# Which three experts are fixed ahead of routing, and a third shared step: 13 expert steps in place of 14

## The reference

```
g_sel = argmax(softmax(xf @ w_rg + b_rg))                 # one group of 4
in_group = e_logits of that group                         # 4 experts
top_w, top_i = top_k(softmax(in_group), 2); top_w /= sum(top_w)
h = silu(xf @ w_g[e]) * (xf @ w_u[e])                     # 1024 -> 256
out = sum over the two e of gate * (h @ w_d[e])           # 256 -> 1024
```

## Time and profile before

| | us |
|---|---|
| median of three runs | 541.12 |
| the profiled execution, its own time | 539.75 |
| its span, first to last instruction | 537.5 |
| TensorE busy | 518.3 (96%) |
| VectorE busy | 259.3 (48%) |
| GpSimd busy | 155.0 (29%) |
| ScalarE busy | 151.2 (28%) |
| granted TensorE clock, mean of the span | 0.993 |

### The profile page before, as it was taken

How to read it: one execution, slowest core, us unless ns; L and a number is a source line. 1 busy time by engine, 2 the same in 40 slices (tenths; PEclk the granted TensorE clock), 3 DMA queues, 4 the chain that set the end, 5 groups by cost and what they waited for, 6 DMA issues and landing times.

```text
span 537.5 us, 7583 instructions
## 1 busy us (share of the span) xinstructions
PE 518.3 (96%) x2798; PEld 322.0 (60%) x2798; DVE 259.3 (48%) x759; ACT 151.2 (28%) x293; POOL 155.0 (29%) x166
## 2 busy tenths in 40 slices
PE   7999999999999999999999999878999999999994
PEld 6777755554455454557544444557887768668841
DVE  3543465543024223342633276576746766663247
ACT  6332497721122222232222315410100111011132
POOL 3016000116000000000310020336777677777310
PEclk8999999999999999999999999999999999999998
DMA  9999997899900000007931022969998999999574
GB/s 289 357 330 353 340 312 312 306 388 370 333 4 1 0 0 1 1 1 284 382 112 64 39 66 87 382 190 402 364 355 282 365 370 364 365 377 368 124 197 179
DMA packets 47417, 126.50 MB, mean 235 GB/s; under 512 B 6654, under 2 KB 19358, under 8 KB 41234
## 3 DMA queue, kind: packets, MB, share of 16 engines
q1 hardware_dynamic: 30912, 99.36, 50.1%
q0 software_dynamic: 11408, 22.05, 15.0%
q10 hardware_dynamic: 5058, 4.58, 2.5%
HBM read 116.48 MB, written 17.30 MB: 249 GB/s over the span
## 4 chain that ended last, share of the span: by engine, by line
PE 82%; DMA 8%; DVE 5%; issue 2%; ACT 1%; POOL 0%; ACTq 0%; SPq 0%; POOLq 0%; DVEq 0%
PE psum L816 78%; DMA f_dram<-arena,add_tok 5%; PE psum L819 3%; DMA u_dram<-arena 2%; DVE arena L2386 1%; DVE x L2391 1%; DMA arena<-f_dram 1%; DMA hy<-in_c_sample_dram 1%; ACT arena L1502 1%; DVE arena L2187 0%; ACT L1502 0%; POOL f_dram L785 0%; DVE arena L2333 0%; ACT hy L1502 0%; POOL uT L774 0%
## 5 line engine op out<-in xcount | busy, mean ns | idle before, releaser
L816 PE MATMUL psum<-ring,uT 128*128 128x512 f32 (+1 forms) x384 | 126.5, 523 | 0.0
L816 PEld LDWEIGHTS psum<-ring,uT 128*128 128x128 f32 (+1 forms) x384 | 56.7, 173 | 60.0 <-issue 55.7
L1502 ACT ACTIVATE arena<-psum 128x512 f32<-128x512 f32 (+6 forms) x80 | 35.7, 476 | 168.2 <-PE psum L816 150.9
L816 PE MATMUL psum<-uT,ring 128*128 128x288 f32 x256 | 64.9, 411 | 0.1
L816 PEld LDWEIGHTS psum<-arena,ring 128*128 128x128 f32 x512 | 58.5, 192 | 5.9 <-issue 3.9
L816 PE MATMUL psum<-arena,ring 128*128 128x128 f32 x512 | 59.2, 276 | 2.7 <-DVE arena L2187 1.8
L754 POOL DMA_INDIRECT arena<-u_dram,part_tok x52 | 53.4, 1027 | 19.9 <-issue 14.3
L816 PEld LDWEIGHTS psum<-uT,ring 128*128 128x128 f32 x256 | 47.9, 190 | 16.2 <-issue 4.0
L816 PE MATMUL psum<-ring,arena 128*64 128x256 f32 (+2 forms) x192 | 50.6, 490 | 0.0
L785 POOL DMA_INDIRECT f_dram<-arena,add_tok x26 | 41.5, 1598 | 23.1 <-DMA f_dram<-arena,add_tok 13.2
L1502 ACT ACT_TABLE_LOAD x33 | 42.3, 1283 | 3.1 <-issue 2.1
(11 more groups left out here) (260 smaller groups left out, 613.4 us busy)
## 6 DMA issues: line engine op xcount, KB each, us to landing
ring<-in_w_mod_dram SPq DMA_DIRECT2D x24, 1024.0 KB, 11.5
ring<-in_w_exp_down_dram SPq DMA_DIRECT2D x12, 1024.0 KB, 13.4
ring<-in_w_exp_gate_dram SPq DMA_DIRECT2D x11, 1024.0 KB, 9.9
ring<-in_w_exp_up_dram SPq DMA_DIRECT2D x11, 1024.0 KB, 12.5
ring<-in_w_in_dram SPq DMA_DIRECT2D x10, 1024.0 KB, 10.2
ring<-in_w_out_dram SPq DMA_DIRECT2D x4, 1024.0 KB, 6.9
uT<-in_w_exp_gate_dram SPq DMA_DIRECT2D x4, 1024.0 KB, 14.2
f_dram<-in_consts_dram POOLq DMA_DIRECT2D x2, 1536.0 KB, 17.0
```

What stands on the lines that cost most here:

```text
L816: return nc.tensor.matmul(out, lhsT, rhs, start=first, stop=last)
L1502: return nc.scalar.activation(out, src, func, **kw).then_inc(done, 1)
```

## The change

Experts 13, 14 and 15 are fixed ahead of routing in place of 0, 1 and 2, and the ranked ones are experts 0 to 12, so column numbers shift by `SORTED` and the offset of `FIRST` goes away. Of the ranked ones, seven run alone and six share three steps, (7, 8), (9, 10) and (11, 12): 13 steps in all. Steps 4, 7 and 10 are pairs, where 5 and 9 were. `NST` and `BIG` (9, now 7) follow from the list. `LAST_AT` stays 7, a paired step now. In the new order of weights the 16th late piece is the first gate weights of step 7, in the cell of step 4's; the 28th to 31st are those of the pair in step 10, the 34th the gate weights of step 11.

```diff
-STEPS = [()] * FIRST + [(0,), (1,), (9, 10), (2,), (3,), (4,), (11, 12), (5,), (6,), (7,), (8,)]
+STEPS = [()] * FIRST + [(0,), (7, 8), (1,), (2,), (9, 10), (3,), (4,), (11, 12), (5,), (6,)]
...
                 if a < FIRST:
-                    return slice(a, a + 1)
+                    return slice(SORTED + a, SORTED + a + 1)
...
-                    chosen[at] = sp.value_load(order[0:1, at:at + 1], min_val=FIRST, max_val=NE - 1)
+                    chosen[at] = sp.value_load(order[0:1, at:at + 1], min_val=0, max_val=SORTED - 1)
...
-                          scale=gsl[e % 4][:, e:e + 1])
+                          scale=gsl[e % 4][:, SORTED + e:SORTED + e + 1])
...
-                link(v.tensor_tensor(out=masked, in0=rank1[:, :, FIRST:NE],
+                link(v.tensor_tensor(out=masked, in0=rank1[:, :, 0:SORTED],
...
-                        col = rank1[:, t, e:e + 1] if e < FIRST else ranks[e % 2][0][:, t:t + 1]
+                        col = (rank1[:, t, SORTED + e:SORTED + e + 1] if e < FIRST
+                               else ranks[e % 2][0][:, t:t + 1])
...
-                out=key, in0=bank[6][:, FIRST:NE], scalar=float(NE),
+                out=key, in0=bank[6][:, 0:SORTED], scalar=float(NE),
...
-                    v.tensor_scalar(order, ordf, float(FIRST - 1), None, ALU.add)\
+                    v.tensor_scalar(order, ordf, -1.0, None, ALU.add)\
...
-                    link(v.tensor_tensor(out=masked[:, 0], in0=gsl[e % 4][:, FIRST:NE], in1=mine,
+                    link(v.tensor_tensor(out=masked[:, 0], in0=gsl[e % 4][:, 0:SORTED], in1=mine,
```

More of the change, by code:

```diff
@@ L2460, in take_out @@
                         dve.wait_ge(s_gs[e % 2], 16 * (e // 2 + 1))
-                        v.tensor_scalar(eo[e % 2][:, 512:1024], bank[5], gsl[e % 4][:, e:e + 1],
+                        v.tensor_scalar(eo[e % 2][:, 512:1024], bank[5], gsl[e % 4][:, SORTED + e:SORTED + e + 1],
                                         None, ALU.mult).then_inc(s_eod, 1)
@@ L2556, in _ @@
                         ranks_of(STEPS[NST - 1][0], lastr)
-                        link(v.tensor_tensor(out=masked, in0=gates[:, :, FIRST:NE],
+                        link(v.tensor_tensor(out=masked, in0=gates[:, :, 0:SORTED],
                                              in1=mine.unsqueeze(1)
```

## The result

The changed kernel took 544.34 us in the median of four runs (543.60 to 545.41), the kernel before beside it 540.65 (540.13 to 541.88, four runs): ratio 1.0066, 95% interval 1.0039 to 1.0093. It is slower by 3.6 us, where 538.3 was forecast; the range ended at 543.6. The profiled execution was the longest of the four, 545.41 us, with a span of 543.5.

What follows compares the result with a forecast made beforehand. TensorE, the weight stream and the closing scatter-adds were taken to bind within some 7 us. Of TensorE's 9.3 us, half went in the stream; scatters landing 2.8 us earlier, off the 541.12 median, gave 538.3, range 535.8 to 543.6.

Steps and rivals of the forecast that it cites:

- TensorE's saving: Expert loop: two single steps out, one pair in, 10.8 us off TensorE's path, 9.3 left after VectorE's delay.
- the stall in step 1: Step 1: TensorE's down products wait for VectorE's slot comparisons and hidden values, 1.5 us on TensorE's path.
- The dip closes: DMA share around 399 to 421 us: early rows keep the weight queue full, recovering 3.3 us.
- the piece that mattered: The 34th late weight piece, step 11's gate weights: to land at 486.2 instead of 487.7.
- The prediction's row counts: Rows gathered and scattered up to 487.7 us: 1843 before, 1946 after, 103 more costing 1.8 us of DMA time.
- Step 11's gate weights are the 34th: Step 11's start: TensorE arrives at 482.7, waits for the 34th piece at 486.2; loop ends at 511.8, not 516.66.
- rival 2: Waits before steps 10 and 11: TensorE's clock falls there and the gain shrinks; chance 0.08.
- The tail: Closing scatter-adds: first issued at 499.2, last landing at 512.6 instead of 515.36, moving the finish 2.8 us earlier.
- Rival 1: Expert loop: stream keeps up, TensorE's saving arrives, end at 507.4, 3.8 to 5 us won, 536.5; chance 0.15.
- Rival 3: Weight stream: the DMA hole stays, 34th piece at 489.5, scatters land at 515.8, 541.1 us; chance 0.20.
- Rival 4: Step 10: the pair's scatters take 9.6 us each in the full stream, 545.3 us, or half, 543; chance 0.13.

Runs made afterwards that it cites:

- The first experiment: Changed kernel with a single step's wait for its up weights moved down to just ahead of the up products: 538.83 us, ratio 0.9954 against the kernel before.
- the fillers: Changed kernel with 26 filler products of 128 columns in TensorE's wait ahead of step 11: 541.50 us, ratio 1.0008 against the kernel before.
- the lighter stream: Only the first half of each expert's down weights loaded from step 3 on: changed kernel 532.02 us, kernel before 539.73 us.

## Why the prediction was wrong

The forecast stood at 539.75 - 2.8 = 536.95 us for a profiled execution; the one of after took 545.41, 8.5 us more. Step by step, in order of time:

1. **The start of the loop**, 1.4 us later than in the profile before. Not part of the change; the same code varies by some 3 us between profiles.
2. **TensorE's saving and the stall in step 1.** Right in kind, the stall priced at about twice its size. Step 1 took 386.81 - 375.07 = 11.7 us against 11.06 before; the stall was 0.7 to 0.9 us, where 1.5 was put down. The second pair shows no wait over 0.2 us.
3. **The dip closes.** Right for the most part (0.95 for 0.81 and 1.03 for 0.96: 2.2 of the 3.3 us). **But the piece that mattered did not come sooner**, the first step that failed. It was put at 486.2 and landed, less the later start, at 488.0: 1.8 us late. The 31st, put at 475.4, landed at 451.89 + 26.3 = 478.2, less the later start 476.8, so the wait before step 10 was 2.81 us and not 0.9. Over the stretch from the loop's start to that landing the weight queue moved 37.86 MB after and 37.12 before, in 127.3 and 127.1 us, GpSimd's queue 7.78 and 7.42 MB. More was moved, but the pieces up to the 34th are the same bytes: as far as the two starts are alike, the 0.74 MB belong to pieces behind it. The last piece did come sooner: 477.97 + 26.3 = 504.3, 142.3 us after the loop's start, before 145.3. The prediction moved all landings by one amount, and here only the last came sooner. Whether the filled dip did that is open, for with the fixed experts alone it was filled too, and the last came only 0.6 us sooner. The 34th was issued 97.0 us after the loop's start, 12 us sooner than before (109.0), with nine loads in flight in place of five, itself among them, and landed at the same time. Why the packets of later pieces go ahead was not tested.

   The prediction's row counts don't follow from its own list of steps: 1843 and 1946 are 1912 and 2082 by it, or 1856 and 1968 without the rows of step 0, which are gathered ahead of the late loads. The latter are 112 rows apart, 1.9 us in place of 1.8, and what GpSimd's queue moved more, 0.36 MB, is 1.5 us at the prediction's 4.1 us per MB: this term was not the error. What was not there is the 3.3 us for the dip, taken in full off the 34th piece.
4. **"Step 11's gate weights are the 34th"**: the step that decided. It is true, and not enough: `expert_in` waits at its head for gate and up weights, so the step hangs on the 35th, issued 3 us behind. 3.15 us. It could be read in the code and in the earlier trace rows, where five pieces are 3.6 us each. With that piece the same sum gives a start of step 11 at 486.2 + 3.6 = 489.8, the scatters 13.0 us behind it, and with the 12.06 us that after's scatters took from there (507.70 to 519.76) a last landing at 514.9: 515.36 before, no change. So this piece alone takes away the gain; that the kernel is slower comes from items 3 and 5 on top. The first experiment shows this step: with the wait moved, the kernel is 5.5 us faster than the changed one, the clock's 2 us among them.
5. **The clock** was rival 2, at a chance of 0.08, against it that "each is short"; the forecast's sum has nothing for it. One wait was 6.44 us. The rows then show 0.69 over 487 to 498 and the 32 gate products at 5.87 us instead of 3.8: 2.1 us, measured again by the fillers. The chance was far too small, and the clock adds to the late piece instead of standing in its place. The Trainium skill, page TensorE: Matmul & The Clock Gate, section Part 1: The HAM clock gate, has the array go back to 1.2 GHz in idleness and up again under work; this trace agrees, with 0.69 over the stretch of the wait and its end and 1.00 from 498 on.
6. **The tail.** Step 11's start is 1.8 + 3.15 + 0.1 = 5.0 us late, the first scatter with the clock 7.1. From there the forecast had 13.4 us to the last landing, measured 12.06: the scatters found a quiet DMA, 1.3 us won. The loads of f_dram took 5.96 instead of 4.40 us, 1.6 more. In the profiles of the variants it is anything from 4.2 to 5.9, and nothing in the change explains it.

Sum: 1.4 + 5.0 + 2.1 - 1.3 + 1.6 = 8.8, less 0.3 outside the span: 8.5. The first and the last term, the loop's start and the loads of f_dram, vary from profile to profile whatever the kernel. Without them 5.8 us are left, and the medians are 544.34 - 538.3 = 6.0 from the forecast.

**The rivals.** Rival 1, the stream keeps up, is what the kernel does with the lighter stream (a gain of 7.7 us, not there with the full one). Rival 3 is refuted in its cause, for the dip closed, but not in what it fed into the sum: it had the 34th piece no sooner, at 489.5, and at 488.0 the piece landed nearer to that than to the forecast's 486.2. Rival 4 was to carry the other sign and did not: it wanted the pair's scatters at 9.6 us each, and they took 4.5 to 4.8. It had 543 to 545.3 us, close to what was measured, by the wrong mechanism. The right one was not among the rivals: a wait in the first line of a step, on a piece that the step doesn't need yet. The chance of 0.14 for slower was too small for a kernel in which three bounds lie within 7 us, and the relief of one brings the next wait with its own costs.

What is left open: item 3's order within the queue, how often the clock falls at a wait of 2 to 4 us, and the loads of f_dram.

## What to carry to other kernels

Where a change makes an engine arrive earlier at a stream, list every semaphore that the first instruction of the step waits for, and take the last of them; then move each wait down to its first use, which cost nothing here and was worth 5.5 us. Test the stream first by making it lighter: if the changed kernel gains 12 us and the one before 1, the saving is real and the stream eats it. An idle gap on TensorE also has to be priced with the products behind it at half clock, unless another wait for the same stream follows, which may absorb them, as one profile here suggests.

## What the runs showed of the hardware

- The granted clock did not fall only behind the wait of 6.4 us. Behind waits of 2.98, 3.2, 3.5 and 3.8 us it fell too; behind 1.55, 2.1, 2.3 and 2.81 it did not; and where waits of 3.7 and 3.3 us stood 11 us apart, it fell behind the second alone.
- 26 useless products in a wait made the kernel 2.8 us faster than the same kernel idling there.
- In the changed kernel an indirect scatter-add of one half took 9.1 to 11.2 us from issue to landing while 1 MB loads were queued (twenty of them, issued from 382 to 487) and 4.5 to 4.8 us with the stream over (the last four).
- With nine 1 MB loads of one queue in flight, itself among them, a load landed 30 us after its issue, with five 18 us (the 34th after and before); with 2.2 and 2.6 us of idle DMA time filled, the 34th landed 127.3 us after the loop's start in the changed kernel and 126.5 in the one with only the fixed experts changed, 127.1 before.
